# Block attention's queries and keys of the first mixer from seven products of quarters

## What is computed

```python
def nsa_moba_mixer(x, positions, w_in, w_out, ...):
    proj = x @ w_in                      # 256 x 1024 by 1024 x 2840
    qa, kc, vc, ksl, vsl, kw, vw, ga, qm, km, vm = jnp.split(proj, EVEN_SPLITS, axis=-1)
    ...
    o_a = nsa_attention(...)             # compressed, selected and window attention
    o_b = moba_attention(rope(heads(qm, 8), positions), rope(heads(km, 8), positions), heads(vm, 8))
    return jnp.concatenate([o_a, o_b], axis=-1) @ w_out
```

## Time and profile before

| | |
|---|---|
| median of 3 runs | 1143.73 us (1143.28 to 1144.44) |
| profiled execution | 1144.65 us, of which span 1142.9 us |
| TensorE busy | 1058.1 us, 93% of the span |
| VectorE busy | 401.9 us, 35% |
| ScalarE busy | 221.1 us, 19% |
| chain that ended last | TensorE 67%, DMA 23%, VectorE 6% |
| granted TensorE clock, mean | 0.984 |

### The profile page before, as it was taken

One profiled execution on the slowest core, in us unless ns is written; L12 is line 12 of the kernel. 1 busy time (PEld: TensorE's weight loads), 2 busy tenths in 40 slices (PEclk: granted clock), 3 DMA queues, 4 the chain that ended last, 5 costly groups with the idle time before them and its releaser, 6 DMA issues.

```text
span 1142.9 us, 15878 instructions
## 1 busy us (share of the span) xinstructions
PE 1058.1 (93%) x6490; PEld 527.8 (46%) x6490; DVE 401.9 (35%) x1070; ACT 221.1 (19%) x509; POOL 1.0 (0%) x6
## 2 busy tenths in 40 slices
PE   9999999999999999999999999987878897789996
PEld 6555455554786455554655544423222332224231
DVE  5776463114556654114736734101100010001003
ACT  2045341111024432111131522101000000001011
POOL 0000000000000000000000000000000000000000
PEclk9999999999999999999999999999988999899999
DMA  9878478977943378996836738999999999999995
GB/s 320 185 199 292 174 266 357 421 329 251 339 163 132 122 275 346 421 381 208 322 130 228 290 136 290 386 430 425 428 429 426 428 430 427 428 430 428 399 424 231
DMA packets 84997, 363.66 MB, mean 318 GB/s; under 512 B 23138, under 2 KB 28612, under 8 KB 61892
## 3 DMA queue, kind: packets, MB, share of 16 engines
q1 hardware_dynamic: 84132, 362.59, 81.3%
q10 hardware_dynamic: 800, 0.17, 0.1%
HBM read 361.69 MB, written 1.05 MB: 317 GB/s over the span
## 4 chain that ended last, share of the span: by engine, by line
PE 67%; DMA 23%; DVE 6%; ACT 1%; issue 1%; SPq 1%; DVEq 0%
DMA weights<-in_expert_w_down_dram 16%; PE bank L1471 13%; PE bank L1025 6%; PE bank L1003 6%; PE bank L1535 5%; PE bank L1583 5%; DMA weights<-in_expert_w_up_dram 4%; PE bank L1515 4%; PE bank L1684 3%; PE bank L1015 2%; PE bank L1812 2%; PE bank L1403 2%; PE bank L1957 2%; PE bank L1242 2%; DMA weights<-in_expert_w_gate_dram 1%; PE bank L1917 1%
## 5 line engine op out<-in xcount | busy, mean ns | idle before, releaser
L1471 PE MATMUL bank<-weights,mixed 128*32 128x512 f32 x992 | 226.3, 610 | 31.3 <-DMA weights<-in_expert_w_gate_dram 17.9
L1471 PEld LDWEIGHTS bank<-weights,mixed 128*32 128x32 f32 x992 | 63.1, 112 | 181.1 <-issue 169.6
L1025 PE MATMUL bank<-weights,mixed 128*128 128x512 f32 x192 | 89.8, 602 | 0.0
L1003 PE MATMUL bank<-weights,x_transposed 128*128 128x512 f32 x192 | 89.2, 601 | 0.0
L1535 PE MATMUL bank<-weights,work 128*32 128x512 f32 x464 | 62.1, 670 | 25.5 <-DMA weights<-in_expert_w_down_dram 21.0
L3098 DVE TENSOR_TENSOR work<-work,bank 64x512 f32<-64x512 f32 (+1 forms) x22 | 15.0, 682 | 157.7 <-PE bank L1471 156.0
L2285 ACT ACTIVATE work<-bank 128x512 f32<-128x512 f32 (+1 forms) x32 | 19.0, 594 | 229.5 <-PE bank L1535 190.7
L3000 DVE COPY work<-bank 64x512 f32<-64x512 f32 (+1 forms) x30 | 20.7, 690 | 117.0 <-PE bank L1535 75.1
L1684 PE MATMUL bank<-work,heads_transposed 128*128 128x512 f32 x120 | 56.0, 607 | 4.6 <-ACT work L2285 4.6
L1471 PE MATMUL bank<-weights,projected 128*64 128x256 f32 x512 | 57.0, 381 | 0.0
L3005 DVE COPY work<-bank 128x256 f32<-128x256 f32 (+1 forms) x22 | 10.8, 493 | 127.4 <-PE bank L1487 127.4
(11 more groups left out here) (464 smaller groups left out, 1405.8 us busy)
## 6 DMA issues: line engine op xcount, KB each, us to landing
weights<-in_expert_w_gate_dram SPq DMA_DIRECT2D x28, 2048.0 KB, 16.9
weights<-in_expert_w_up_dram SPq DMA_DIRECT2D x28, 2048.0 KB, 17.7
weights<-in_expert_w_down_dram SPq DMA_DIRECT2D x24, 2048.0 KB, 19.1
weights<-in_moe_w_down_dram SPq DMA_DIRECT2D x16, 2048.0 KB, 14.7
weights<-in_moe_w_gate_dram SPq DMA_DIRECT2D x14, 2048.0 KB, 13.0
weights<-in_moe_w_up_dram SPq DMA_DIRECT2D x12, 2048.0 KB, 15.2
weights<-in_sb_w_in_dram SPq DMA_DIRECT2D x6, 2048.0 KB, 19.5
weights<-in_w_in_dram SPq DMA_DIRECT2D x6, 2048.0 KB, 16.2
```

Source lines behind the costliest of these rows:

```text
L1003: i = mm(BANK[bank or 6 + t][:, :], XT[:, kt, t * P:(t + 1) * P], w[:, kt, :], start=kt == 0, stop=kt == KT - 1)
L1025: i = mm(BANK[bank][:, :], mixT[:, kt, t * P:(t + 1) * P], w[:, kt, :], start=kt == 0, stop=kt == KT - 1)
L1471: i = mm(b[n_slots * c:n_slots * (c + 1), e * F:(e + 1) * F], x[:, kt, q * n_slots:(q + 1) * n_slots], extra_weights(c, kt) if outside els ...
```

## The change

Chunks 4 and 5 (now keys first, then queries) also become seven products of quarters, 28 pieces for 32. Products 1 (lower features by keys) and 2 (upper features by keys) are plain. Products 3, 5, 6, 7 and 4 follow in that order, 5, 6, 7 and 4 with weight sums `MW1` to `MW4`. Those are written over the weights themselves (`MW1` over the lower queries, and so on), and banks 6 and 7 are used in turn. The token sums `AS`, which lay in the room of the transposed heads, move to the norm parameters' room; so the load of the first norm rows moves behind the first expert stage's third chunk load. Both chunks count as done only after product 4 (`chunk_done` + 2). The scale of the queries moves from the bank copy into the copy of the transposed heads. The core of the diff:

```diff
-        AS = [quarter(QK[:, 1024 + CH * i:1024 + CH * (i + 1)]) for i in range(4)]
+        AS = [quarter(NORM_[:, CH * i:CH * (i + 1)]) for i in range(4)]
+        KM_LO, KM_HI = (slot(N_AB + 4)[:, at:at + HALF_SLOT] for at in (0, HALF_SLOT))
+        QM_LO, QM_HI = (slot(N_AB + 5)[:, at:at + HALF_SLOT] for at in (0, HALF_SLOT))
+        MW1, MW2, MW3, MW4 = QM_LO, QM_HI, KM_LO, KM_HI
...
                         load_unit_chunk(0, j)
+                        if L == 0 and j == 2:
+                            load_norm(0, (a["ln_mix_g"][0], a["ln_mix_b"][0]))
...
-            project_half(N_AB + 4, 0, 0, 4)
+            def product_6(k0, k1):
+                if k0 == 0:
+                    pe.wait_ge(half_copied, 2)
+                    pe.wait_ge(sums_ready, 6)
+                i = pieces(6, AS[1], MW2, k0, k1)
+                if k1 == KT // 2:
+                    i.then_inc(products_psum, 1)
...
+            pieces(6, lo[:, :, 0:P], KM_LO).then_inc(half_psum, 1)
...
-            project_half(N_AB + 4, 0, 4, 8)
+            pieces(7, hi[:, :, 0:P], KM_HI).then_inc(products_psum, 1)
...
-                project_half(N_AB + 4, 1, 0, 3)
+                pieces(6, AS[3], QM_HI, 0, 3)
...
-                project_half(N_AB + 4, 1, 3, 8)
+                pieces(6, AS[3], QM_HI, 3, 4).then_inc(half_psum, 1)
+                pe.wait_ge(sums_ready, 5)
+                pieces(7, AS[0], MW1).then_inc(products_psum, 1)
...
-            project_half(N_AB + 5, 0, 0, 2)
+            product_6(0, 2)
...
-                1: lambda: (cmp_keys(), project_half(N_AB + 5, 0, 3, 5)),
-                2: lambda: (cmp_score(), project_half(N_AB + 5, 0, 5, 7)),
-                3: lambda: project_half(N_AB + 5, 0, 7, 8),
+                1: lambda: (cmp_keys(), product_6(3, 4)),
+                2: lambda: (cmp_score(), product_7(0, 2)),
+                3: lambda: product_7(2, 3),
+                4: lambda: (product_7(3, 4), cmp_transpose()),
+                5: lambda: product_4(0, 1),
+                6: lambda: product_4(1, 2),
+                7: lambda: product_4(2, 4),
+                8: lambda: project_half(N_AB + 6, 0, 0, 2, 7),
...
-            take_moba_half(3, 0)
...
+            act.wait_ge(half_psum, 1)
+            act.wait_ge(proj_copied, 3)
+            ac(AU, BANK[6][:, :], ACT.Copy).then_inc(half_copied, 1)
...
-            take_moba_half(3, 1)
+            act.wait_ge(half_psum, 2)
+            ac(pj[:, 0, C_QM:C_QM + CH], BANK[6][:, :], ACT.Copy).then_inc(half_copied, 1)
+            act.wait_ge(products_psum, 7)
+            ac(pj[:, 1, C_QM:C_QM + CH], BANK[7][:, :], ACT.Copy).then_inc(proj_copied, 1)
...
+            dve.wait_ge(half_copied, 1)
+            dve.wait_ge(products_psum, 6)
+            tt(km0, AU, BANK[7][:, :], ALU.add)
+            weights_loaded(N_AB + 4)
+            weights_loaded(N_AB + 5)
+            tt(MW1, QM_LO, KM_LO, ALU.subtract).then_inc(sums_ready, 1)
...
-            rope_moba(3, 0)
+            dve.wait_ge(sums_ready, 5)
+            dve.wait_ge(half_psum, 2)
+            tt(MW2, QM_HI, MW1, ALU.subtract).then_inc(sums_ready, 1)
...
+            dve.wait_ge(sums_ready, 6)
+            tt(MW3, MW2, KM_LO, ALU.subtract).then_inc(sums_ready, 1)
+
+            def after_product_5():
+                dve.wait_ge(half_copied, 2)
+                dve.wait_ge(proj_copied, 4)
+                tt(qm0, qm0, BANK[7][:, :], ALU.add).then_inc(sums_ready, 1)
+                tt(MW4, MW2, KM_HI, ALU.subtract).then_inc(sums_ready, 1)
+
+            def after_product_6():
+                dve.wait_ge(products_psum, 8)
+                link(tt(AU, AU, BANK[6][:, :], ALU.add))
+                tt(qm0, qm0, AU, ALU.add).then_inc(sums_ready, 1)
...
+            def after_product_7():
+                dve.wait_ge(products_psum, 9)
+                link(tt(AU, AU, BANK[7][:, :], ALU.add))
+                tt(qm1, qm1, AU, ALU.add).then_inc(sums_ready, 1)
...
+            def after_product_4():
+                dve.wait_ge(chunk_done, N_AB + 6)
+                tt(km1, AU, BANK[6][:, :], ALU.subtract).then_inc(proj_copied, 1)
...
-            attention(AB_JOBS, 0, 0, {1: keys_copy, 2: cmp_softmax_in, 3: cmp_softmax_out, 5: lambda: rope_moba(3, 1), 7: lambda: rope_moba(4, 0),
-                                      10: lambda: rope_moba(4, 1),
+            attention(AB_JOBS, 0, 0, {0: after_product_5, 1: keys_copy, 2: lambda: (cmp_softmax_in(), after_product_6()), 3: cmp_softmax_out,
+                                      4: lambda: rope_moba(3, 0), 5: after_product_7, 6: lambda: rope_moba(3, 1), 7: lambda: rope_moba(4, 0),
+                                      8: after_product_4, 10: lambda: rope_moba(4, 1),
```

More of the change, by code:

```diff
@@ L142 @@
 OUT_DMAS = 3
-SB_SUMS = 7
-SB_PRODUCTS = 7
-AB_SUMS = 4
-AB_PRODUCTS = 5
+SB_SUMS = 14
+SB_PRODUCTS = 11
+AB_SUMS = 11
+AB_PRODUCTS = 9
 AGAIN_VAR = (3, 13)
@@ L1280, in _, with pieces, product_7, product_4 @@
             product(5, AS[0], AW1).then_inc(chunk_done, 3)
-            project_half(N_AB + 4, 0, 0, 4)
+            def pieces(bank, x, weights, k0=0, k1=KT // 2):
+                w = quarter(weights)
+                for kt in range(k0, k1):
+                    i = mm(BANK[bank][:, :], x[:, kt, :], w[:, kt, :], start=kt == 0, stop=kt == KT // 2 - 1)
+                return i
+            def product_6(k0, k1):
[5 more added lines that the diff above has]
+                    i.then_inc(products_psum, 1)
+            def product_7(k0, k1):
+                if k0 == 0:
+                    pe.wait_ge(proj_copied, 4)
+                    pe.wait_ge(sums_ready, 8)
+                i = pieces(7, AS[2], MW3, k0, k1)
+                if k1 == KT // 2:
+                    i.then_inc(products_psum, 1)
+            def product_4(k0, k1):
+                if k0 == 0:
+                    pe.wait_ge(sums_ready, 10)
+                i = pieces(6, hi[:, :, P:S], MW4, k0, k1)
+                if k1 == KT // 2:
+                    i.then_inc(chunk_done, 2)
+            pe.wait_ge(proj_copied, 1)
+            chunk_loaded(N_AB + 4)
+            pieces(6, lo[:, :, 0:P], KM_LO).then_inc(half_psum, 1)
             pe.wait_ge(roped, 2)
```

41 lines of the change are left out of this document (20 added, 21 removed).

## The result

The changed kernel takes **1151.51 us** (median of 5 runs, 1151.14 to 1153.19) where the kernel before took 1143.73: 7.8 us slower, ratio 1.0073 (95% interval 1.0058 to 1.0087). Forecast were 1149.7, with a range of 1145.8 to 1153.0. (A piece is one 128x512 matmul, which the trace shows as two records.)

The account below looks back on a forecast made before the run. TensorE was taken to bound the mixer, its delay handed on to the end. Waits of 10.0 us, less 3.44 for pieces and 0.5 for a swallowed wait, gave about +6.0: 1143.73 + 6.0 = 1149.7 us, range 1145.8 to 1153.0.

Parts of the forecast that it names:

- Direction, bound and mechanism: First mixer: TensorE full, VectorE's added work between minima holds back its scores; slower given 0.83.
- The pieces, -3.44 us: TensorE's projections in the mixer: four 128x512 pieces fewer at 0.86 us each, 3.44 us saved.
- The first rival: VectorE's added work hides and TensorE keeps its 3.44 us: 1140.3 us; 7 in 100.
- The sums ahead of the attention, at nothing: VectorE before the attention: one 128x512 sum and MW1 to MW3, 7.6 us, fit in 7.9 us of room.
- ScalarE, 1.1 us: Ahead of product 6, TensorE waits for ScalarE to copy the window keys, then empty bank 6: +1.1 us.
- VectorE in the attention: Up to job 10's scores: 8.8 us added, 2.3 us refilled from idle time; TensorE waits of 0.7 to 1.7 us.
- Two of the signs: Between 60 and 95 us: TensorE waits on VectorE of some 9 us; VectorE at 9.5 or more of 10.
- The forecast's own walk: Both engines stepped forward in written order using timeline durations; job 10's scores come 7.7 us late, 6.0 after later pieces.
- Transfers, at nothing: First expert stage's second gate and first up chunk loads go out at about 89 us, 3 us later, costing nothing.
- granted clock 1.00 throughout the mixer: A sign listed for the profile after: TensorE's clock does not fall anywhere in the mixer.
- a rival that comes on top: The clock falls once or twice in the mixer, +1.7 to +3.4 us: 1151.4 to 1153.1; 13 in 100.
- The rule on PSUM: Tiling speeds TensorE's compute but not bank emptying, so the saving is worth only what the emptying engine lets through.

Follow-up runs that it names:

- Placed anew: Changed kernel with the same work on every engine in another order, bank 6 emptied ahead of the window keys' copy; 1141.93 us.
- six idle matmuls: Changed kernel plus six unused 128x512 matmuls on TensorE: one ahead of product 6, two in step 1, one each in steps 3, 4 and 7; 1150.36 us.
- MW4 short: Changed kernel with the last weight sum (MW4) made over only 64 of its 2048 columns; 1147.85 us.
- bank 6 first: Changed kernel with ScalarE emptying bank 6 ahead of its copy of the window keys instead of behind it; 1149.87 us.
- four idle matmuls: Changed kernel plus four unused 128x512 matmuls on TensorE, ahead of product 6 and in steps 1, 3 and 7; 1149.76 us.
- one idle matmul: Changed kernel plus one unused 128x512 matmul on TensorE, ahead of the scores of job 2; 1149.93 us.

## Why the prediction was right or wrong

**Direction, bound and mechanism: right.** VectorE's added work inside the attention costs TensorE more than four pieces save; this was tried from both sides (its work left out: level; its work alone on the old kernel: as slow as the change).

**The pieces, -3.44 us:** right in size, and worth nothing in this order (four put back: no slower). Placed anew, 2.8 of it are kept. The first rival had its condition too wide: with the scores of job 10 late by 1.7 us the kernel would only have come out level, and to keep all 3.44 they would have had to come 1.7 us early.

**The sums ahead of the attention, at nothing:** right. TensorE had no wait on MW1, and the first minima waited 1.83 us for TensorE, not for MW3.

**ScalarE, 1.1 us:** right. The trace's 0.96 counts from the modelled end of the instruction before; from start to start it is 1.10 (59.34 to 60.44), and 1.2 when taken away.

**VectorE in the attention:** six waits at full clock within 0.1 to 0.2 us of those forecast, the other two within 0.3, each a little shorter. Without the fall of the clock the loss is 5.7 us, the forecast's 6.0. Two of the signs were off all the same: in the changed kernel the waits on VectorE come to 5.1 us in four places and not some 9, as the slow stretch lies over the others, and VectorE was never at 9.5 of 10 throughout from 60 to 95 us. Even at full clock, with six idle matmuls, it was at 8.07 and 8.40 between 60 and 80. The forecast's own walk leaves VectorE idle there, 1.2 us at the compression scores and from 61.9 to 63.4 ahead of job 0's minima, so that sign did not fit the walk.

**Transfers, at nothing:** right. The two loads that were expected at about 89 went out at 89.0 and 89.4, and TensorE has no wait on a transfer in the first expert stage.

**The step that failed:** "granted clock 1.00 throughout the mixer". The clock stood at half for 10.2 us, which costs 1.95 us. I had it as a rival that comes on top, +1.7 for one fall and 1151.4 in all, with 13 in 100, because my longest new gap (1.7 us) was no longer than the gap of 1.71 us after which the clock had held. That compared one gap with one gap, and the same stage of the kernel before has a longer one, of 2.30 us, behind which the clock stayed at 1.00:

```profile
877.28 3.64 PE L1535 MATMUL bank<-weights,work 128*32 128x512 f32 x32 [2.30 <-DMA weights<-in_expert_w_down_dram]
```

So the length of one gap did not decide there either. That the price came out close (1.7 against 1.95) is luck: the 1.70 were those of about 3.4 us at half clock (0.51, 0.50, 0.50 and 0.78 in the four microseconds from 897 us on) in a stretch where TensorE had nothing to wait for. In the mixer 3.4 us at half cost nothing and 10.2 us cost 1.95, by another mechanism (last section).

**The rule on PSUM** (the Trainium skill, Trainium Kernel Development and Optimization, section Best Practices) pointed to the right engine. The trace puts two limits to it. Of the 8.8 us that VectorE does in the attention only the four sums that read a bank, 2.8 us, are emptying; MW4, the rope half and the two sums that add into the queries are not. And with the same work on VectorE, 2.8 of 3.44 us are kept in another order, so at this amount of work the order decided what the saving was worth.

## What to carry to other kernels

Where one engine is relieved by work on another, walk both forward in their written order over the stretch where they meet; idle time on the helper counts only where it lies behind the right instruction. An item added between an instruction that frees a bank and the one that refills it can be on the path one for one, as MW4 was (2.06 of 2.2 us); put it where the full engine has independent work queued. And when new waits come close together on TensorE, allow for a fall of its clock on top, even if gaps as long have left it up before. Beside another full engine, as here, the fall costs not the time at half clock but the delay of an instruction that the other engine waits for.

## What was not expected of the hardware

The clock fell from 1.00 to 0.50 at about 67.6 us after waits of 0.96 us (until 60.44) and 1.42 us (until 67.37), both shorter than gaps that had left it up elsewhere (1.71 us and the 2.30 us above). In the same profile waits of 0.81, 1.23 and 1.57 us between 83 and 97 us left it at 1.00, and so did one of 1.53 us at 73.54 in the kernel with MW4 short. The wait of 0.96 us is not what it takes: with bank 6 first and with four idle matmuls it is gone and the clock fell, with MW4 short it is there and the clock stayed. What the profiles have in common stands in the table. In the six where the clock fell between 67 and 72 us, TensorE had waited 1.14 us or more for VectorE right ahead of the compression scores; in the five where it stayed up, the kernel before among them, 0.58 us or less. The nearest pair is four and six idle matmuls, which up to there differ by one matmul in step 1 alone: 1.14 us and a fall, 0.36 us and none. Why waits there count and longer ones elsewhere don't stays open.

The Trainium skill (TensorE: Matmul & The Clock Gate, section HAM oscillation) tells of a kernel in which each burst of matmuls behind a wait for a load started at half clock. Behind three such waits in the last expert stage of the kernel before that was so for one (1.94 us) and not for two (1.71 and 2.30 us); the fall in the mixer came behind waits on VectorE.

A fall need not cost anything. Each of the changed kernels in which the clock fell lost as much as the fall lengthened the compressed keys and the compression scores, for which VectorE waits. The sixteen score matmuls take 1.97 us at full clock, as with four idle matmuls, where the fall began behind them:

```profile
69.54 1.97 PE L1364 MATMUL bank<-misc,heads_transposed 128*128 128x32 f32 x16
```

They took 3.62 us in the changed kernel (and the compressed keys 0.79 instead of 0.48), 3.51 in its repetition and 3.00 with one idle matmul: 1.96, 1.54 and 1.03 us more. Over the +5.70 of the kernel without a fall these three lie by 1.95, 1.54 and 1.03. The slow projection pieces behind the scores cost nothing, since TensorE would have waited for VectorE in that time.
